# Two-layer block on one core: position-bias tiles built pair by pair, and three edits of waits and passes around TensorE

## What is computed

```python
s_own = (jnp.einsum('bhqd,bhnd->bhqn', q_c, k_own).astype(jnp.float32) * scale
         + table[:, rel_bucket(d_own)])
s_own = jnp.where(d_own >= 0, s_own, NEG_INF)
p = jax.nn.softmax(logits, axis=-1).astype(v.dtype)
```

## Time and profile before

| | us |
|---|---|
| median of 3 runs | 782.49 |
| lowest and highest | 782.23, 783.82 |
| the profiled execution, its own time | 784.3 |
| its span in the trace | 782.5 |
| its mean granted clock | 1.0 |

### The profile page before, as it was taken

One profiled execution on the slowest core, in us unless ns is written; L12 is line 12 of the kernel. 1 busy time (PEld: TensorE's weight loads), 2 busy tenths in 40 slices (PEclk: granted clock), 3 DMA queues, 4 the chain that ended last, 5 costly groups with the idle time before them and its releaser, 6 DMA issues.

```text
span 782.5 us, 12013 instructions
## 1 busy us (share of the span) xinstructions
PE 771.3 (99%) x4640; PEld 683.1 (87%) x4640; DVE 568.2 (73%) x916; ACT 439.1 (56%) x609; POOL 151.0 (19%) x112
## 2 busy tenths in 40 slices
PE   9999999999999999999999999999999989999998
PEld 8787778888888899999998889999799878978886
DVE  5755565894558678878784469899875896898785
ACT  6854675345444566566563363566656344889751
POOL 0002930000000004444543000534105000007000
DMA  9986544344455465455455536437475416554311
GB/s 339 406 308 230 168 155 162 112 159 162 161 170 207 163 206 203 175 175 203 164 199 179 212 113 228 144 113 255 157 248 183 162 55 215 199 179 161 108 55 54
DMA packets 23364, 141.77 MB, mean 181 GB/s; under 512 B 3692, under 2 KB 4600, under 8 KB 7440
## 3 DMA queue, kind: packets, MB, share of 16 engines
q1 hardware_dynamic: 20160, 134.51, 48.5%
q0 software_dynamic: 1376, 3.43, 1.3%
q10 hardware_dynamic: 1776, 3.10, 1.1%
HBM read 139.96 MB, written 2.64 MB: 182 GB/s over the span
## 4 chain that ended last, share of the span: by engine, by line
PE 77%; DVE 9%; DMA 7%; ACT 2%; issue 2%; POOL 1%; SPq 0%; ACTq 0%; DVEq 0%
PE gemm L497 14%; PE gemm L499 14%; PE gemm L498 14%; PE gemm L503 9%; PE gemm L505 9%; PE gemm L504 9%; DMA raw<-in_weights 3%; DMA bias_rows<-bias_row 3%; DVE wlo L1733 2%; DVE xc L2320 1%; ACT whi L1198 1%; PE head L561 1%; POOL wsum_p L2515 1%; PE head L794 1%; DMA bias<-bias_rows 1%
## 5 line engine op out<-in xcount | busy, mean ns | idle before, releaser
L1733 DVE TENSOR_TENSOR wlo<-raw,whi 128x2048 fp32r<-128x2048 f32 x119 | 277.5, 2333 | 92.8 <-ACT whi L1198 92.5
L1198 ACT CAST whi<-raw 128x2048 fp32r<-128x2048 f32 x120 | 228.9, 1908 | 196.5 <-PE gemm L499 107.7
L497 PE MATMUL gemm<-whi,x0hi 128*128 128x512 f32 (+2 forms) x368 | 145.0, 394 | 0.7 <-DVE wlo L1733 0.7
L499 PE MATMUL gemm<-whi,x0lo 128*128 128x512 f32 (+2 forms) x368 | 141.5, 385 | 0.0
L498 PE MATMUL gemm<-wlo,x0hi 128*128 128x512 f32 (+2 forms) x368 | 141.2, 384 | 0.0
L503 PE MATMUL gemm<-x1hi,whi 128*128 128x256 f32 x400 | 113.6, 284 | 0.1
L505 PE MATMUL gemm<-x1hi,wlo 128*128 128x256 f32 x400 | 113.2, 283 | 0.0
L504 PE MATMUL gemm<-x1lo,whi 128*128 128x256 f32 x400 | 113.2, 283 | 0.0
L497 PEld LDWEIGHTS gemm<-whi,x0hi 128*128 128x128 f32 x368 | 69.1, 188 | 15.5 <-issue 2.0
L499 PEld LDWEIGHTS gemm<-whi,x0lo 128*128 128x128 f32 x368 | 69.1, 188 | 13.6
L498 PEld LDWEIGHTS gemm<-wlo,x0hi 128*128 128x128 f32 x368 | 69.2, 188 | 12.2
(11 more groups left out here) (377 smaller groups left out, 1342.2 us busy)
## 6 DMA issues: line engine op xcount, KB each, us to landing
raw<-in_weights SPq DMA_DIRECT2D x122, 1024.0 KB, 4.8
raw<-in_weights SPq DMA_DIRECT2D x4, 512.0 KB, 6.3
bias_rows<-bias_row POOLq DMA_DIRECT2D x1, 1536.0 KB, 20.8
memt<-in_memt SPq DMA_DIRECT2D x4, 256.0 KB, 5.3
tok<-in_mem SPq DMA_DIRECT2D x1, 1024.0 KB, 7.2
xt<-in_xt SPq DMA_DIRECT2D x2, 512.0 KB, 11.0
xres<-in_x ACTq DMA_DIRECT2D x1, 1024.0 KB, 9.1
bias<-bias_rows POOLq DMA_DIRECT2D x8, 128.0 KB, 4.4
```

The source lines that it names most:

```text
L497: mm(o, xh, wh, start=start, stop=False)
L499: return mm(o, xl, wh, start=False, stop=stop)
L1198: nc.scalar.copy(whi[:, p % RING, :], raw[:, p % RING, :]).then_inc(s_hi, 1)
L1733: V.tensor_tensor(wlo[:, p % RING, :], raw[:, p % RING, :], whi[:, p % RING, :].bitcast(F32), ALU.subtract).then_inc(s_lo, 1)
```

## The change

Four edits, none of which alters what is computed.

1. **Bias tiles.** The write of 128 copies is cut into four DMAs of two heads (384 KB each). POOL issues one, waits for it, issues the two loads of that pair, and goes on to the next pair. Each pair has a semaphore of its own, and DVE waits for a pair's ahead of its even head.
2. **mLSTM turn.** A new semaphore `ml_turned_read` is raised by DVE's second read of the bank head2; PE's next turn waits for it in place of `ya_ready`. DVE's own wait ahead of the gate product is for the same semaphore in place of its general order semaphore.
3. **Keep-awake.** 12 products in place of 16.
4. **First product.** ACT signals `first_input_hi` after the first of the two `x1hi` tiles of the first pair; PE starts with the two products that need only that tile, and waits for the pair before the third. For this the order within each group of four goes over the token halves innermost.

```diff
@@ -863,7 +865,7 @@
             def ml_turn(h):
                 pe.wait_ge(s_mn, h + 1)
                 if h >= 1:
-                    pe.wait_ge(s_mya, h)
+                    pe.wait_ge(s_mread, h)
                 for j in range(2):
                     for t in range(T):
                         i = nc.tensor.transpose(A[2][:, j * S + t * P:j * S + t * P + P],
@@ -1012,7 +1014,7 @@
             def keep_awake():
 
                 pe.wait_ge(s_memset, 1)
-                for _ in range(16):
+                for _ in range(12):
                     mm(A[2][:, 0:P], ones[:, :], ones[:, :], start=True, stop=True)
 
             def first_pieces():
@@ -1022,10 +1024,15 @@
                     for half in range(2):
                         pair = (2 * p + half) % 4
                         pe.wait_ge(s_hi if half else s_hi0, p + 1)
-                        pe.wait_ge(s_inhi, pair + 1)
+                        if (p, half) == (0, 0):
+                            pe.wait_ge(s_in0, 1)
+                        else:
+                            pe.wait_ge(s_inhi, pair + 1)
                         order_ = [(t, 2 * pair + j, slice((2 * half + j) * 512, (2 * half + j) * 512 + 512))
-                                  for t in range(T) for j in range(2)]
+                                  for j in range(2) for t in range(T)]
                         for t, kb, ws in order_:
+                            if (p, kb, t) == (0, 1, 0):
+                                pe.wait_ge(s_inhi, 1)
                             mm(o[t][:, :], x1hi[:, kb, t * P:t * P + P], whi[:, p % RING, ws], start=kb == 0, stop=False)
                         pe.wait_ge(s_lo if half else s_lo0, p + 1)
                         for t, kb, ws in order_:
@@ -1299,6 +1306,8 @@
                         act.wait_ge(s_xt[i // 2], 16)
                     for kb in (2 * i, 2 * i + 1):
                         last = nc.scalar.activation(hi[:, kb, :], src[:, kb, :], ACT.Copy, scale=pcol(col, kb))
+                        if name == "mem" and kb == 0:
+                            last.then_inc(s_in0, 1)
                     last.then_inc(s_inhi, 1)
 
             def split_half(p, h):
@@ -2000,8 +2009,8 @@
                 else:
                     n = SMAX.index(j)
                     if kind == "moba":
-                        if h == 0:
-                            dve.wait_ge(s_bias, 16 * MOBA_H)
+                        if h % 2 == 0:
+                            dve.wait_ge(s_bias[h // 2], 32)
                         V.scalar_tensor_tensor(pr[:, 0:P], scores[:, 0:P], 0.125, bias[:, h, P:S],
                                                ALU.mult, ALU.add)
                         order(V.scalar_tensor_tensor(pr[:, P:TRI], scores[:, P:TRI], 0.125, bias[:, h, :],
@@ -2143,7 +2152,8 @@
                         blk = 2 * h + j
                         i = V.scalar_tensor_tensor(xc[:, blk, :], A[2][:, j * S:j * S + S], pcol("head_g", blk),
                                                    xc[:, blk, :], ALU.mult, ALU.add)
-                    order(i)
+                    i.then_inc(s_mread, 1)
+                    dve.wait_ge(s_mread, h + 1)
                     V.tensor_tensor(xc[:, 2 * h:2 * h + 2, :], xc[:, 2 * h:2 * h + 2, :],
                                     zm[:, 2 * h:2 * h + 2, :], ALU.mult).then_inc(s_mya, 1)
 
@@ -2469,13 +2479,14 @@
             pool.wait_ge(s_rbs, 1)
             pool.dma_start(rows_out, brows[0:MOBA_H, :]).then_inc(s_rbd, 16)
             pool.wait_ge(s_rbd, 16)
-            pool.dma_start(scratch.rearrange("h (p n) -> h p n", p=P),
-                           rows_out.unsqueeze(1).broadcast_to([MOBA_H, P, TRI])).then_inc(s_rbd, 16)
-            pool.wait_ge(s_rbd, 32)
-
-            for h in range(MOBA_H):
-                pool.dma_start(bias[:, h, :], scratch[h, P - 1:P - 1 + P * (TRI - 1)]
-                               .rearrange("(p n) -> p n", p=P)[:, 0:S]).then_inc(s_bias, 16)
+            for k in range(MOBA_H // 2):
+                pair = slice(2 * k, 2 * k + 2)
+                pool.dma_start(scratch[pair, :].rearrange("h (p n) -> h p n", p=P),
+                               rows_out[pair, :].unsqueeze(1).broadcast_to([2, P, TRI])).then_inc(s_rbd, 16)
+                pool.wait_ge(s_rbd, 32 + 16 * k)
+                for h in (2 * k, 2 * k + 1):
+                    pool.dma_start(bias[:, h, :], scratch[h, P - 1:P - 1 + P * (TRI - 1)]
+                                   .rearrange("(p n) -> p n", p=P)[:, 0:S]).then_inc(s_bias[k], 16)
 
             pool.wait_ge(s_rc, 32)
             for s_, c in ((3, 3), (4, 4)):
```

More of the change, by code:

```diff
@@ L294, in program @@
         s_xt = [s_xt, sem("x_columns_loaded_2")]
+        s_in0 = sem("first_input_hi")
         s_gain, s_onehot = sem("gains_loaded"), sem("onehot_loaded")
@@ L299, in program @@
             "squares_summed", "turned", "turned_hi", "turned_lo"))
-        s_rb, s_rbs, s_rbd, s_bias = (sem(n) for n in (
-            "rel_rows", "rel_rows_copied", "rel_rows_stored", "bias_loaded"))
+        s_rb, s_rbs, s_rbd = (sem(n) for n in ("rel_rows", "rel_rows_copied", "rel_rows_stored"))
+        s_bias = [sem(f"bias_loaded_{k}") for k in range(MOBA_H // 2)]
         s_jt, s_jte, s_js, s_jse, s_jx, s_jp, s_jpe, s_jo, s_jn = (sem(n) for n in (
@@ L331, in program @@
         s_rc = sem("rotary_loaded")
+        s_mread = sem("ml_turned_read")
         s_zero, s_wsum = sem("zeros_ready"), sem("window_sums_ready")
```

## The result

| | before | changed |
|---|---|---|
| median, us | 782.86 (6 runs, 782.23 to 783.82) | 798.06 (6 runs, 794.63 to 948.4) |
| the profiled execution, its own time | 784.3 | 794.63 |
| its span | 782.5 | 792.8 |
| its mean granted clock | 1.0 | 0.994 |

The changed kernel is slower: ratio 1.0179, 95% interval 1.0158 to 1.0200. Two of its six runs (902.95 and 948.4 us) had a mean granted clock of 0.79 and 0.75, for which no cause is known; the ratio leaves them out, and the other four lie between 794.63 and 798.22, with a median of 797.35. The prediction was 779.8 us with a range from 779.0 to 781.9, and called faster. It was wrong.

The account below looks back on a forecast made before the run. PE, busy 99% of the span, was taken as the bound, so only its waits pay. Gains of 1.90 + 0.73 + 0.07 = 2.70 us took 784.3 to 781.6, less 1.8 to the median: 779.8 us, range 779.0 to 781.9.

Parts of the forecast that it names:

- The copy of a quarter: Bias chain on POOL: each two-head copy takes 8.6 us, a fixed 4.5 plus 4.1; bounds 5.2 and 20.8.
- The upper bound of 20.8: Bias copies: no gain at all from the smaller size, so a quarter takes 20.8 us like the whole.
- The rotation: POOL's work behind the bias chain: starts 3.1 us late, ends at 107.0, costs nothing under a cover of some 7 us.
- The slower rival: Bias copies hardly get faster; PE waits for the last pair from 14.7 us a copy; 804.3 us at 20.8; chance 0.04.
- the 12 KB store of 4.5 us: Store ahead of the bias copy, POOL waited 4.52 us: taken as the copy's fixed part and as evidence against slow copies.
- The bias stall: PE's turn of the probabilities at 76.93: earlier bias tiles give PE back 1.90 us, from 1.5 to 1.93.
- The mLSTM turn: PE's mLSTM turns follow DVE's second read of the bank: 0.73 us gained, counted once; bounds 0 and 1.46.
- The start: First products begin about 0.5 us earlier, but only 0.07 us is kept; bounds 0 and 0.13.
- Cold first products: Rival at the start: after fewer keep-awake products PE stays at the lower clock, losing 2.0 us, 781.9 us; chance 0.12.

Follow-up runs that it names:

- the pairs wide: Changed kernel with the 128 repetitions instead of the 2 heads as outermost loop of each pair's copy: 782.39 us, ratio 0.9992 against before.
- second execution of before: The kernel before, unchanged, profiled once more: 782.73 us, span 780.9, with no wait for the bias loads left.

## Why the prediction was wrong, step by step

**The copy of a quarter, 8.6 us: wrong, and the step that failed.** Measured 18.3, 16.3, 14.4 and 13.9. I took a fixed part and bytes at one rate, from two rows of other sizes. The copy's shape also changed, and it decides: 2 engines in place of 8. The upper bound of 20.8 was right as a bound. The choice between the ends was made by size, when the row of 1536 KB was the nearer in what counted. By its rows the copy of before moved some 75 GB/s (1536 KB in 21.1 us), where the second slice of time on the profile's page, at a DMA share of 9 tenths, has 406: with the weights running beside the copy, that was reason to ask how many engines worked on it. It was not asked.

**The rotation, 3.1 us late under a cover of some 7: a wrong size, and never worked out at the other end.** The place was named, with the right reader; the price was taken only at 8.6 us a copy. GpSimd needs 19.7 us for the whole rotation once all chunks are there (109.20 to 128.91), and PE came to its turn at 118.2 (129.08 - 10.86). So it decides from 42.0 + 4 x (T + 1.1) + 19.7 = 118.2, that is from T = 13.0 us. With the measured mean of 15.7 us the left side is 128.9, a wait of 10.7 us, where 10.86 was measured. The slower rival put the point at 14.7, and its place at the last pair of bias tiles.

**The slower rival, with 0.04: right in its cause ("something other than bytes sets their time"), wrong in its place.** It foresaw 24.5 us at 20.8 for each copy. With the measured mean of 15.7 us its own sum gives 42.0 + 4 x 16.8 + 5.8 = 115.0 for the last pair against 110.9, so 4.1 us for PE; measured was 0.88. DVE's timeline has the addition of that pair, and PEld's its first score:

```profile
113.70 0.29 DVE L2014 SCALAR_TENSOR_TENSOR prob<-head,bias 128x128 f32<-128x128 f32 x1 [5.06 <-DMA bias<-bias_rows]
```

```profile
109.86 0.30 PEld L722 LDWEIGHTS head<-qk_t 64*128 64x128 f32 x4 [0.17 <-issue]
```

The tiles came 1.3 us earlier than that sum, and they were needed later: the first score is at 109.86, so the addition was due at 110.8 and not at 108.5, because the last two distances from pair to pair were 14.05 us each (81.76, 95.81, 109.86) and not 12.9. Its evidence against, the 12 KB store of 4.5 us, only showed the fixed part.

**The bias stall, 1.90 us of gain: the mechanism was right, its use against the median was not.** In the profiled execution of the changed kernel the second pair's score is at 81.76 against 83.65 before; the stall is gone. But it was one execution's. The prediction took 1.8 us off for the distance to the median and the same stall off once more. The stall was the distance. With the pairs wide, everything else as in the change, 782.39 is what was left, where the prediction had 779.8.

**The mLSTM turn, 0.73 us once: right.** Gaps of 0.76 and 1.23 us in the changed kernel, and 0.7 us to the end in seven traces:

```profile
647.20 0.42 PEld L871 LDWEIGHTS head<-ident,qk_t 128*128 128x128 f32 x4 [0.76 <-issue]
...
654.14 0.42 PEld L871 LDWEIGHTS head<-ident,qk_t 128*128 128x128 f32 x4 [1.23 <-issue]
```

**The start, 0.07 us: not to be told from nothing.** The first product stood at 6.55, where I had 6.75, and the second half's remainder at 10.77, where I had 10.8.

**Cold first products, 781.9: did not happen.** After 12 passes the first four products take one row of 0.77 us, as before:

```profile
6.55 0.77 PEld L1036 LDWEIGHTS gemm<-whi,x1hi 128*128 128x128 f32 x4
```

The clock was lost elsewhere, behind the new stall. The changed kernel's stretches around it (columns as above):

```profile
116.00:120.00 4.00, 1.82 (x14) 0.84 (x12) 2.66 (x4) 2.98 (x10) 3.84 (x4) 1.00 0.11 16
120.00:124.00 4.00, 0.00 (x0) 0.00 (x0) 1.28 (x2) 3.09 (x5) 3.92 (x6) 0.82 0.62 246
124.00:128.00 4.00, 0.00 (x0) 0.00 (x0) 0.00 (x0) 0.00 (x0) 3.84 (x7) 0.50 0.00 0
...
130.00:132.00 2.00, 2.00 (x6) 1.61 (x6) 1.76 (x2) 0.00 (x0) 0.00 (x0) 0.50 0.00 0
132.00:134.00 2.00, 2.00 (x8) 1.59 (x8) 1.46 (x2) 0.00 (x0) 0.00 (x0) 0.81 0.00 0
134.00:136.00 2.00, 2.00 (x10) 1.66 (x9) 0.00 (x0) 0.00 (x0) 0.00 (x0) 1.00 0.81 258
```

A value of 0.50 is the lower of the two levels, 1.2 GHz. PE stood still from 118.2, the clock fell during it, and it was 1.00 again from 134, with PE at work since 129.1. From the turn L700 to L768 it is 143.74 - 129.08 = 14.66 us. The second execution of before has the same stretch on PEld's timeline:

```profile
117.66 0.47 PEld L698 LDWEIGHTS head<-ident,tok 128*128 128x128 f32 x4
...
130.67 0.63 PEld L766 LDWEIGHTS head<-prob_t,tok 128*64 128x64 f32 x8 [0.35 <-issue]
```

That is 13.01 us, so the lower clock cost 1.65 us. In the kernel with the bias edit alone, after 12.17 us of idle, the stretch took 15.04 us: 2.0 us.

**The ledger.** The changed kernel's span against that of the second execution of before, 792.8 - 780.9 = 11.9 us: the stall 10.86, the clock 1.65, the turn of the probabilities 0.7 (0.88 less the usual 0.17 of issue), less 0.7 for the mLSTM, less 0.18 for a first score at 68.65 instead of 68.83. These make 12.3; the 0.4 left are a shorter wait for `wlo` near 555 us (567 in the changed kernel; 0.43 against 0.91 us), which scatters between 0.41 and 0.91 us in the traces with and without the change. The median of the four runs, 797.35, lies 2.7 us above this profiled execution; the bias edit alone had 796.76 to 797.77. What made the other three of the changed kernel 2.2 to 3.6 us longer was not seen, since only this one has a trace.

## What to carry to other kernels

Before a DMA is cut into smaller ones, look at what its outermost loop becomes: if the cut takes that loop from 8 to 2, each part keeps the full load of one DMA engine and is hardly faster than the whole (13.9 to 18.3 us against 18.7 to 21.1). Then price what stands in the same engine's program behind the chain at both ends of the unknown duration, not only at the chosen one; here the tiles that the edit was about cost 0.7 us and the rotation behind them 10.9. And when one profiled execution lies above the median, ask first whether the stall that is to be removed is that distance; a second profile of the same kernel answers it.

## What the runs showed of the hardware

- A copy from DRAM to DRAM issued by GpSimd with 2 as its outermost count moved 51 to 55 GB/s at 0.12 to 0.13 of the 16 DMA engines, some 27 GB/s for an engine. With 4, 8 and 128 outermost it moved 105, 205 and 323 GB/s when nothing else ran. With 128 outermost, the same 384 KB took 5.2 to 8.5 us in place of 13.9 to 18.3.
- The granted clock fell to 0.50 during an idle time of 10.9 us, stayed there until 132 at least, and was 1.00 again from 134, with PE at work since 129.1; 1.65 us were lost. Behind an idle time of 1.93 us it did not fall (24 products in 5.35 us, as elsewhere).
- DVE waited 2.50 us for the bias tiles and PE lost 0.1 us; at 4.31 us PE lost 1.93, at 5.06 us 0.88 and at 5.46 us 0.80. (The last two include 0.17 us that PEld stands there in any case.) The cover differs from pair to pair, so one pair's can't be used for another.
